# Two requests moved on TensorE's queue: a mean of squares to the end of the first column set, a norm's spread one output tile later

## What is computed

```python
def rms_norm(x, g):
    y = x * rsqrt(mean(x * x, axis=-1, keepdims=True) + EPS)
    return y * g

def chunked_sgu(x, g_norm, w_in, g_v, w_s, b_s, w_out):      # mixer A
    h = rms_norm(x, g_norm)
    z = gelu(h @ w_in)
    u, v = split(z, 2, axis=-1)
    v = rms_norm(v, g_v)                                     # in chunks of 128 tokens, 8 groups
    sv = einsum("gts,bnsgc->bntgc", tril(w_s), v) + b_s
    return (u * sv) @ w_out

x = x + chunked_sgu(x, ...)
x = x + conv_ffn(x, ...)          # begins with rms_norm(x, f_norm)
```

## Time and profile before

| | us |
|---|---|
| Median of 3 runs | 1947.44 |
| Lowest and highest of them | 1944.9, 1947.74 |
| The profiled execution | 1943.98 |
| Its span, first to last instruction | 1942.2 |
| TensorE busy within the span | 1914.9 |
| VectorE busy | 1492.3 |
| ScalarE busy | 931.3 |

### The profile page before, as it was taken

How to read it: one execution, slowest core, us unless ns; L and a number is a source line. 1 busy time by engine, 2 the same in 40 slices (tenths; PEclk the granted TensorE clock), 3 DMA queues, 4 the chain that set the end, 5 groups by cost and what they waited for, 6 DMA issues and landing times.

```text
span 1942.2 us, 27731 instructions
## 1 busy us (share of the span) xinstructions
PE 1914.9 (99%) x9704; PEld 1626.4 (84%) x9704; DVE 1492.3 (77%) x2181; ACT 931.3 (48%) x1631; POOL 451.8 (23%) x323
## 2 busy tenths in 40 slices
PE   8999999999999999999999899999999999999999
PEld 8988878878888888888999888878788888888887
DVE  7366758988888876887854788889988887876875
ACT  6242535544444444444513888766444444444443
POOL 0000001333332310011111545542333332301010
PEclk9999999999999999999999999999999999999999
DMA  5111233122212249971111000030221222269681
GB/s 178 44 44 44 92 125 108 66 87 87 86 67 95 90 147 305 275 172 35 44 44 44 34 23 23 12 131 26 105 87 65 97 82 80 83 248 304 183 173 66
DMA packets 63401, 199.06 MB, mean 102 GB/s; under 512 B 5200, under 2 KB 5584, under 8 KB 56144
## 3 DMA queue, kind: packets, MB, share of 16 engines
q1 hardware_dynamic: 48656, 163.29, 24.1%
q0 software_dynamic: 14656, 34.61, 8.2%
HBM read 162.22 MB, written 35.65 MB: 102 GB/s over the span
## 4 chain that ended last, share of the span: by engine, by line
PE 89%; DVE 6%; ACT 2%; issue 2%; DMA 1%; SPq 0%; POOL 0%; ACTq 0%; DVEq 0%
PE banks L2272 28%; PE banks L2274 28%; PE banks L2273 28%; PE banks L2644 1%; DVE xT L1808 1%; DVE xT L1815 1%; DVE fw_lo L1766 1%; PE banks L2618 1%; PE banks L2619 1%; PE banks L2394 1%; PE banks L2606 0%; DVE small L2167 0%; DVE pT_lo L2113 0%; DMA b<-c_scratch 0%; ACT lg_later L1372 0%
## 5 line engine op out<-in xcount | busy, mean ns | idle before, releaser
L2272 PE MATMUL banks<-t_hi,fw_hi 128*128 128x512 f32 x1248 | 488.2, 391 | 5.0 <-DVE t_lo L1722 1.5
L2274 PE MATMUL banks<-t_hi,fw_lo 128*128 128x512 f32 x1248 | 485.9, 389 | 0.0
L2273 PE MATMUL banks<-t_lo,fw_hi 128*128 128x512 f32 x1216 | 473.4, 389 | 0.0
L2272 PEld LDWEIGHTS banks<-t_hi,fw_hi 128*128 128x128 f32 x1248 | 234.3, 188 | 58.6 <-DVE t_lo L1722 3.1
L2274 PEld LDWEIGHTS banks<-t_hi,fw_lo 128*128 128x128 f32 x1248 | 234.3, 188 | 48.9
L2273 PEld LDWEIGHTS banks<-t_lo,fw_hi 128*128 128x128 f32 x1216 | 228.3, 188 | 47.4 <-issue 0.5
L709 POOL TENSOR_TENSOR nrm<-raw 128x512 f32<-128x512 f32 x40 | 55.7, 1392 | 725.8 <-DVE fw_lo L1766 431.0
L2272 PE MATMUL banks<-fw_hi,fw_hi 128*128 128x512 f32 x544 | 211.8, 389 | 1.1 <-DVE fw_lo L1925 1.1
L2274 PE MATMUL banks<-fw_hi,fw_lo 128*128 128x512 f32 x544 | 211.8, 389 | 0.0
L2273 PE MATMUL banks<-fw_lo,fw_hi 128*128 128x512 f32 x544 | 211.7, 389 | 0.0
L1213 ACT ACTIVATE fw_hi<-b 128x512 fp32r<-128x512 f32 x154 | 97.1, 631 | 227.0 <-PE banks L2274 215.2
(11 more groups left out here) (211 smaller groups left out, 4167.5 us busy)
## 6 DMA issues: line engine op xcount, KB each, us to landing
raw<-in_w_f_in SPq DMA_DIRECT2D x44, 1024.0 KB, 5.0
c_scratch<-xT SPq DMA_DIRECT2D x44, 512.0 KB, 2.7
b<-c_scratch SPq DMA_DIRECT2D x16, 1024.0 KB, 10.0
a_sum<-in_w_f_out POOLq DMA_DIRECT2D x16, 1024.0 KB, 14.0
raw<-in_w_f_out SPq DMA_DIRECT2D x54, 256.0 KB, 11.0
w_raw<-in_w_ao SPq DMA_DIRECT2D x16, 512.0 KB, 3.7
x_scratch<-xT SPq DMA_DIRECT2D x4, 2048.0 KB, 7.8
xT<-x_scratch SPq DMA_DIRECT2D x8, 1024.0 KB, 18.7
```

Of the source, the lines that this page charges most:

```text
L2272: nc.tensor.matmul(out, w_h, m_h, start=start, stop=False, **kw)
L2273: nc.tensor.matmul(out, w_h, m_l, start=False, stop=False, **kw)
L2274: return nc.tensor.matmul(out, w_l, m_h, start=False, stop=stop, **kw)
```

## The change

Two edits, both in TensorE's list. Other engines' lists stay as they are.

```diff
             pe.wait_ge(ones_done, 1)
-            columns(0, h_hi_a, h_lo_a, 0, {(1, 5): lambda: mean(0, 0, 7)}, True)
+            columns(0, h_hi_a, h_lo_a, 0, {(1, 7): lambda: mean(0, 0, 7)}, True)
...
             o_tile(0, 1, True)
             mean(1, 0, ADDED[1] + 8)
             o_tile(1, 1)
+            o_tile(0, 1)
             spread(1, 0)
-            loop(5, 3, o_counts, lambda i: o_body(1))
+            o_tile(1, 1)
+            loop(6, 2, o_counts, lambda i: o_body(1))
```

## The result

The changed kernel takes 1949.67 us (median of 16 runs, 1948.64 to 1950.86), the kernel before 1945.17 us in as many (1944.05 to 1947.74). The ratio is 1.0021, with a 95% interval of 1.0015 to 1.0028: 4.1 us slower, 2.9 to 5.4. (The medians lie 4.5 us apart.

The account below looks back on a forecast made before the run. TensorE, busy 99% of the span, was taken to bound the kernel, so only its waits count. +2.88 and -1.39 give +1.49 us, on the median of before 1948.9 us; range 1946.6 to 1951.8 us.

Parts of the forecast that it names:

- rival A: Behind the second mean: TensorE's clock falls in the longer wait, costing 2.2 us more, +3.7 us in all; chance 0.34.
- Term 1: From first to second mean: the VectorE and ScalarE chain starts 24 matmuls later, lengthening TensorE's wait; +2.88 us.
- Its passing on to the end: Behind the second mean: nothing absorbs the delay, so TensorE carries its 2.88 us to the end.
- Term 2: At the spread: tile dt = 2 goes ahead of it, so TensorE's wait there is gone; -1.39 us.
- rival C: Around the moved spread: tile dt = 2 or 3 waits as long, taking the gain; 1950.3 us, chance 0.07.
- Rival B: At the first mean: it does wait in unprofiled executions, so moving it costs nothing; 1946.0 us, chance 0.06.

Follow-up runs that it names:

- the second edit alone: Kernel before with one more output tile ahead of the spread, the mean of squares in its old place; 1944.93 against 1945.76 us, ratio 0.9993.
- the second trace of before: The kernel before, unchanged, profiled once more; one execution, 1945.63 us.

## Why the prediction was right, and where not

The measured 1949.67 us lies in the range, and 4.1 us (2.9 to 5.4) is just beyond the 3.9 us that were called the bound of what can be told, with an interval that holds both sides of it; the chance for a result beyond it was given as 0.20. What happened is rival A, not the forecast.

**Term 1, the delay of the chain: right.** Forecast 2.88 us and the second mean at 41.41; measured 2.98 at the first link and 2.97 at the second mean, which started at 41.50 (0.1 us of it stood ahead of the first mean already). The wait was to be some 3.9 us, and is 3.92. That the chain is what counts, and not the place of the first mean, is shown from both sides: with 72 matmuls beside the chain the waits at the mean are gone, once with the first mean in its old place and once in the new.

**Its passing on to the end: right.** With the wait filled by 24 matmuls the chain is as late as in the changed kernel, and the way from the second mean to the FFN's first mean is no longer than before (219.87 and 219.91 us): so ScalarE's later GELUs hold nobody up, and the delay is neither made good nor added to. The statement that the next weights would be ready before TensorE wants them held only thanks to the new wait; without that wait they cost 1.08 us.

**Term 2: right to 0.01 us in the traces.** 1.39 us forecast; 1.39 in the changed kernel and in the second edit alone. No wait has taken its place, as rival C would have it. By the times alone (0.9984 to 1.0002) the gain could also be nothing.

**Rival B: ruled out.** Where the first mean comes later and the second keeps its place, the kernel is slower, by 5.1 us behind k = 7 and 2.1 behind k = 6; where it comes earlier 0.9 us is gained behind it in the trace. The changed kernel's trace has no idle mark at the first mean either.

**The step that failed is the weighing of rival A**, 0.34 against the forecast's 0.50. Its mechanism was right, and its price nearly: 24 slow matmuls were forecast, and 27, 18 and 14 stand in the three traces of it (the window of 43.0 to 48.6 us above has 28 rows with the last one of the mean; in all three the mean ahead of them is slower too, 1.53 to 1.87 us and not 1.05); 2.2 us, at most 2.6, were forecast and 3.0, 2.5 and 2.2 measured. The prediction took the price from the start of the program, where all of the slow stretch that it could see lies on work. The level there was read from the spacing of the matmuls alone; the granted clock of 6 to 11 us is written as 1.00, but the spacing, 0.213 us, is that of the stretch which is written as 0.50 in the changed kernel. What was wrong is the argument from the trace of before, that a wait of 1.3 us is harmless and one of 6.2 a state of rest, with 3.9 between the two and so open. The clock falls at the wait of 3.9 us in all three traces, and also at that of 2.48 us in both traces that have it. Rival A's forecast of +3.7 us lies between the two comparisons (+4.5 and +3.1 us by the medians, +4.1 and +2.9 by the ratios).

The Trainium skill's rule, page "TensorE: Matmul & The Clock Gate", section "What's actually happening", that an idle stretch brings the slow clock back, is borne out here: the granted clock is 0.50 from 43.0 to 48.6 us, behind the wait. Had the prediction gone by it, 1951.1 us would have been the forecast.

**An error in the prediction's base.** The profiled execution of before, 1943.98 us, is one without the wait in the first FFN and without the slow clock in attention. The median of three runs, 1947.44, was high; that of 16 is 1945.17. The predicted difference was put on top of the high one. On 1945.17 the forecast would have been 1946.7 us and rival A's 1948.9. That the number 1948.9 came near the measured one is owed to this, not to the forecast's mechanism. So is the place of the measured time inside the range: moved down by the same 2.27 us the range would end at 1949.5 us, a little under 1949.67. That it lies there was luck.

## What to carry to other kernels

Where an engine asks for something and comes back for what follows from it, the place of the request counts as much as the place of the wait: the time to watch is the chain between the two against the work that lies beside it, and an early request without an idle mark may be what sets a later wait. A wait on TensorE can cost more than its length, if the clock falls at it: at this place it fell at waits of 2.48 and 3.9 us in all five traces and at those of 1.04 us in none of five, and 12 matmuls moved between request and wait made the difference. And a change of a few us is best read between marks that both traces have, since the whole time here differs from run to run by as much.

## What was not expected of the hardware

The clock need not fall while TensorE waits. At the waits of 2.48 us it fell only behind them: the mean's small matmuls and the next four, or two in the other trace, still started at full speed, and then came 3.4 us at half. At the waits of 3.9 us it fell 1.9 and 1.1 us before the end of the wait in two traces and 0.4 us behind it in the third, for 6.8 us each time. So a wait can be paid for later than where it stands, and the same wait costs more or less by how much of the slow stretch meets work. Whoever looks only at the first matmul behind a wait can miss it.

The clock also falls where no wait is longer than 1.3 us. In the attention stage of all 13 traces TensorE waits for 1.04 us and then, after 1.2 us of work, for 1.1 us; in the second trace of before these waits end at 1098.97 and 1101.31 us. In six of the traces the clock falls there, between 0.4 us before and 0.3 us behind the end of the second wait:

```profile
1101.10:1104.50 3.40, 3.19 (x12) 2.93 (x13) 2.26 (x11) 1.72 (x3) 2.81 (x3) 0.50 0.00 0
```

In the other seven it stays at 1.00 beside the same two waits, and at a wait of 1.3 us some 9 us ahead of the first it stays so in all 13. The cost is 1.1 us, in some executions and not in others. The Trainium skill's page "TensorE: Matmul & The Clock Gate" tells of a related case in its section "A second HAM failure mode: psum-queue depth-cycling": in a kernel that goes round the PSUM banks in each iteration, short idle times between groups of matmuls are frequent enough to make the clock swing. These rows agree with it in that the clock fell without a long wait. But here it is a single fall, and that the nearness of the two waits brought it about is not shown.
